# A four-pair opening with two panels side by side in a two-layer hybrid decoder step, on one core

## The chip, the cores and the metric

One core of a Trainium2 chip runs the whole program. The metric is the device time of one execution in microseconds (us); three runs of the kernel before are shown below, and one execution was taken by the profiler.

## What is computed

A decoder trunk of two layers runs one step for 512 prompt tokens and 32 sample tokens (8 sequences of 4). Layer 0 mixes tokens by sliding-window attention with 12 query and 4 key heads, layer 1 by a short gated convolution; in both, 4 further heads attend into 256 memory tokens, and an MLP with a squared ReLU follows. The part that the change touches makes the keys and values of the prompt's memory, for both layers:

```python
def _mem_kv(mem, g, w_kv, k_g):
    n = mem.shape[0]
    kv = _rms_norm(mem, g) @ w_kv
    mk = kv[..., :X_DIM].reshape(n, N_MEM, N_X_HEADS, HEAD_DIM)
    mv = kv[..., X_DIM:].reshape(n, N_MEM, N_X_HEADS, HEAD_DIM)
    return _rms_norm(mk, k_g), mv
```

All inputs are float32 and the products keep nearly that precision: each operand is split into a rounded part (hi) and the rest (lo), and each product is three matmuls (hi·hi, hi·lo, lo·hi).

## The kernel before

Weights stream through a staging buffer `stage` of two places d = 0, 1; a place holds 1,024 KB (8 chunks k of 128 rows by 256 columns). A weight "quad" q is two such loads, so (q, d) names one. ScalarE (ACT) copies a place to `w_hi` (L1389, L1394), VectorE (DVE) subtracts to get `w_lo` (L909 to L912), and the semaphores `w_his[d]` and `w_los[d]` count these. SyncE (SP) issues the next load of a place when `w_los[d]` says that the last one is used up (L449 to L455).

**The opening.** The 256 memory tokens, feature-major in `memx` (8 chunks of 128 by 256), are scaled by the norm's gain and split by `memory_hi` on ACT (L1675) and `memory_lo` on DVE (L1259). Quad 0 holds layer 0's key and value weights, quad 1 those of layer 1. A panel (l, p) of TensorE (PE), in `memory_panel` (L531), is layer l, token half tb = p % 2, and place d = p // 2: p = 0, 1 give keys, p = 2, 3 values. It runs over 8 chunks with three matmuls each, 24 in all, of 256 columns, and adds up in `zps[p % 2][:, 0, 0:256]`, the first of a slot's two banks; so panel p waits (`z_free`) until ACT has taken panel p - 2 out. The norm's factor is left out of the products and multiplied in when a panel is taken: ACT squares the 8 chunks (L1735), DVE adds them in three steps (L1282), PE sums over the partitions in `memory_sums` (L553, called inside panel (0, 0) before its last two chunks), ACT takes the root (L1740), DVE inverts it (L1285), and `take_memory` on ACT (L1687) scales each panel out of its bank.

**The orders written out by hand.** SP issues two loads of memory (512 KB each) and then the two places of quad 0 (L444 to L447). ACT (L1723 to L1766) loads the first part of the constants `con` (44 KB, L1678), converts 8 chunks, copies quad 0's place 0 in two halves, squares 8 chunks, issues the two loads of the tokens `X`, copies place 1, takes the root, and then goes through a loop over (l, p) in which, in this order, each step converts parts of layer 1's memory, brings out finished keys, takes a root of key norms, scales chunks of the tokens (`norm_hi`), takes a panel, copies the next place of weights, and squares tokens. DVE follows with the lo parts in an order of its own (L1268 to L1302). The first engine operation that needs the square root makes ACT load another table of functions. The second part of the constants (443 KB: identity, ones, masks; semaphore `con2`) is issued by ACT after memory's second half has landed (L1728), and PE waits for it before its first panel (L846).

GpSimd (POOL) issues the cached values `vb` when the tokens have landed and the cached keys `kt`, which lie where `memx` lay, after the last use of it (L1886 to L1892). ACT issues the rotary table `cs` in the loop's first step (L1757); POOL needs it for its first rotation (L1893, L1902). SP stores from `vb` (L464, L465) before it goes on with the loads of weights.

After the opening come 12 panels of layer 0's input projection (the first waits for quad 2's `w_los[0]`), attention, the output projection, the MLP, and the same for layer 1.

Of the kernel before, what the change touches and what calls it, by code (L numbers as in the profile page):

```python
# [28 lines left out]
NMEM = 256  # L29
# [37 lines left out]
def build_kernel(nc, xT, memT, wst, cst, rope, swakT, swav, xkT, xv, yT, o_kp, o_vp, o_cp, o_mk, o_mv,  # L67
# [81 lines left out]
    with ExitStack() as ctx:  # L149
# [9 lines left out]
        w_his_half, w_los_half = sem("w_his_half"), sem("w_los_half")  # L159
# [3 lines left out]
        ld = {n: sem("ld_" + n) for n in ("con", "con2", "mem0", "mem1", "x", "x1", "rope", "kt", "vb", "kx0", "kx1", "vx0", "vx1")}  # L163
# [314 lines left out]
        def _(pe):  # L478
# [51 lines left out]

            def memory_panel(l, p):  # L531

                d, tb, slot, q = p // 2, p % 2, p % 2, Q_MEM + l
# [4 lines left out]
                c = l * NMEM + tb * 128  # L538
                for k in range(KC):
                    if (l, p) == (0, 0) and k == KC - 2:  # L540
                        memory_sums()
                    if (l, p) == (0, 0) and k == 0:
                        pe.wait_ge(w_los_half, 1)
                    if (l, p) == (0, 0) and k == KC // 2:
                        pe.wait_ge(w_los[0], 1)
                    if p == 0:
                        pe.wait_ge(m_los[l], k + 1)
                    for i, (w_, r_) in enumerate(((w_hi, 0), (w_hi, 1), (w_lo, 0))):
                        mm = pe.matmul(zps[slot][:, 0, 0:256], act_hl[1][r_][:, k, c:c + 128], w_[:, d, k, :],  # L549
                                       start=(k == 0 and i == 0), stop=(k == KC - 1 and i == 2))  # L550
                mm.then_inc(z_full[slot], 1)

            def memory_sums():  # L553

                pe.wait_ge(m_sum, 3)
# [290 lines left out]
            pe.wait_ge(ld["con2"], 16)  # L846
            for l in range(2):
                for p in range(4):
                    memory_panel(l, p)
# [50 lines left out]
        def _(dve):  # L900
# [1161 lines left out]
```

## Time and profile before

| what | value |
|---|---|
| median of 3 runs | 1170.88 us (1170.84, 1170.88, 1172.97) |
| the profiled execution: its own time | 1172.87 us |
| its span, first to last instruction | 1171.1 us |
| PE busy | 1144.2 us, 98% of the span |
| DVE, ACT, POOL busy | 804.8, 522.4, 132.5 us |
| mean granted TensorE clock | 0.996 |

The profiled execution lies 2.0 us above the median; 1.8 us of it lie outside the span. A difference of 0.2% is 2.3 us.

### The profile page before, as it was taken

The page shows a single profiled execution, that of the slowest core. Times are in us where ns is not written, and L with a number is a line of the kernel's source. Part 1 is how long each engine was busy: PE and PEld are TensorE (multiplying, and loading weights), DVE is VectorE, ACT ScalarE, POOL GpSimd, SP SyncE. Part 2 cuts the span into 40 slices and gives each one's busy share as a digit, 9 for nine tenths or more (in the row PEclk, how much of TensorE's full clock was granted, in tenths as well). Part 3 has the DMA queues.
Part 4 walks back from the last instruction along what each step waited for, and adds up shares of the span by engine and source line. Part 5 has one row for each costly group of instructions (what it writes and reads, how often), then busy time and mean ns, then how long its engine had stood idle before and what let it go on. Part 6 is the DMA issues. An engine that isn't in the chain of part 4 may idle for free.

```text
span 1171.1 us, 22169 instructions
## 1 busy us (share of the span) xinstructions
PE 1144.2 (98%) x8990; PEld 1104.2 (94%) x8990; DVE 804.8 (69%) x1201; ACT 522.4 (45%) x901; POOL 132.5 (11%) x140
## 2 busy tenths in 40 slices
PE   5999899999999999999999999999999999999998
PEld 5899655999999999999999999999999999999998
DVE  6789965798667568558658555589866855856853
ACT  7623767357227326326524222436722722732630
POOL 0038743000000000000141121200000000000000
PEclk9999989999999999999999999999999999999999
DMA  8543150213222312413522322221321332231231
GB/s 333 191 156 118 50 180 1 76 69 114 103 73 102 116 52 91 143 36 108 183 104 73 145 73 73 75 86 59 132 92 66 109 108 72 79 136 39 104 136 48
DMA packets 23146, 120.18 MB, mean 103 GB/s; under 512 B 2708, under 2 KB 6932, under 8 KB 9892
## 3 DMA queue, kind: packets, MB, share of 16 engines
q1 hardware_dynamic: 17892, 100.93, 24.7%
q0 software_dynamic: 1632, 10.54, 2.4%
q10 hardware_dynamic: 3552, 7.74, 1.9%
q8 instruction: 48, 0.79, 0.3%
q14 instruction: 22, 0.18, 0.0%
HBM read 111.29 MB, written 5.69 MB: 100 GB/s over the span
## 4 chain that ended last, share of the span: by engine, by line
PE 88%; DVE 6%; POOL 2%; DMA 2%; ACT 1%; issue 1%; ACTq 1%; DVEq 0%; POOLq 0%
PE zps L498 48%; PE zps L757 25%; PE ops L757 4%; PE zps L745 4%; DVE tmp L974 2%; PE ops L672 1%; PE zps L549 1%; PE tps L642 1%; POOL sm L1874 1%; DVE w_lo L912 1%; DVE sm L1042 1%; DMA tmp<-z 1%; PE zps L596 1%; ACTq L1685 1%; DMA con<-cst 1%
## 5 line engine op out<-in xcount | busy, mean ns | idle before, releaser
L498 PE MATMUL zps<-act_hi,w_hi 128*128 128x272 f32 x1664 | 348.7, 291 | 0.9 <-DVE w_lo L912 0.9
L498 PE MATMUL zps<-act_hi,w_lo 128*128 128x272 f32 x1664 | 344.1, 288 | 0.0
L498 PE MATMUL zps<-act_lo,w_hi 128*128 128x272 f32 x1664 | 343.2, 288 | 0.0
L757 PE MATMUL zps<-xf,wf 128*128 128x272 f32 x2304 | 298.9, 290 | 1.2 <-issue 1.2
L757 PEld LDWEIGHTS zps<-xf,wf 128*128 128x128 f32 x2304 | 294.1, 188 | 1.9 <-issue 1.6
L498 PEld LDWEIGHTS zps<-act_hi,w_hi 128*128 128x128 f32 x1664 | 262.1, 188 | 5.4 <-issue 2.9
L498 PEld LDWEIGHTS zps<-act_lo,w_hi 128*128 128x128 f32 x1664 | 261.5, 189 | 0.0
L498 PEld LDWEIGHTS zps<-act_hi,w_lo 128*128 128x128 f32 x1664 | 260.0, 189 | 0.0
L1387 ACT ACTIVATE w_hi<-w_stage 128x2048 fp32r<-128x2048 f32 (+1 forms) x61 | 114.8, 1883 | 150.8 <-PE zps L498 123.6
L912 DVE TENSOR_TENSOR w_lo<-w_stage,w_hi 128x2048 fp32r<-128x2048 f32 x59 | 137.5, 2331 | 43.2 <-ACT w_hi L1387 43.0
L1387 ACT ACTIVATE wf<-w_sum 128x1024 fp32r<-128x1024 f32 x64 | 67.9, 1061 | 195.2 <-DVE w_sum L930 88.2
L1017 DVE TENSOR_TENSOR tmp<-zps,rstd 128x544 f32<-128x544 f32 x63 | 45.5, 722 | 142.7 <-PE zps L498 116.7
L1874 POOL TENSOR_SCALAR sm<-sm,st 128x256 f32<-128x256 f32 (+2 forms) x55 | 55.0, 1013 | 108.8 <-DVE st L1049 108.7
L1153 DVE TENSOR_TENSOR act_lo<-tmp,act_hi 128x544 fp32r<-128x544 f32 x64 | 46.1, 721 | 20.2 <-ACT act_hi L1387 20.2
L1429 ACT ACTIVATE sm<-sm,st 128x257 f32<-128x257 f32 (+3 forms) x88 | 42.0, 481 | 29.4 <-DVE st L1042 29.4
L1387 ACT ACTIVATE wf<-w_stage 128x1024 fp32r<-128x1024 f32 (+1 forms) x64 | 52.8, 838 | 5.1 <-PE zps L757 5.0
L757 PE MATMUL ops<-xf,wf 128*128 128x272 f32 x384 | 53.7, 289 | 0.0
L757 PEld LDWEIGHTS ops<-xf,wf 128*128 128x128 f32 x384 | 50.4, 188 | 0.0
L943 DVE TENSOR_TENSOR wf<-w_sum,wf 128x1024 fp32r<-128x1024 f32 x32 | 39.2, 1224 | 15.8 <-ACT wf L1387 13.8
L974 DVE RECIPROCAL tmp<-tmp 128x544 f32<-128x544 f32 x12 | 42.6, 3549 | 8.2 <-ACT tmp L1404 8.2
L1247 DVE TENSOR_TENSOR x_res<-tmp,x_res 128x544 f32<-128x544 f32 x63 | 45.7, 726 | 2.2
L1387 ACT ACTIVATE tmp<-zps 128x272 f32<-128x272 f32 x96 | 37.6, 391 | 15.7 <-PE zps L757 14.4
(182 smaller groups left out, 1288.5 us busy)
## 6 DMA issues: line engine op xcount, KB each, us to landing
w_stage<-wst SPq DMA_DIRECT2D x92, 1024.0 KB, 4.9
kx<-xkT POOLq DMA_DIRECT2D x4, 1024.0 KB, 6.4
vx<-xv POOLq DMA_DIRECT2D x4, 1024.0 KB, 6.9
x_res<-xT ACTq DMA_DIRECT2D x2, 1088.0 KB, 7.6
tmp<-z ACTq DMA_DIRECT2D x32, 68.0 KB, 2.1
yT<-x_res ACTq DMA_DIRECT2D x7, 272.0 KB, 2.0
memx<-memT SPq DMA_DIRECT2D x2, 512.0 KB, 4.7
vb<-swav POOLq DMA_DIRECT2D x1, 1024.0 KB, 8.5
```

The costliest lines, as they stand in the source:

```text
L498: mm = pe.matmul(zps[slot][:, h, 0:n], w_[:, d, k, w:w + 128], r_[:, k, c0 + h * n:c0 + (h + 1) * n], start=(j == 0 and i == 0), stop=(j = ...
L745: mm = pe.matmul(zps[slot][:, h, 0:HALF], w_[:, d, k, w:w + 128], r_[:, k, h * HALF:(h + 1) * HALF], start=(k == 0 and i == 0), stop=(k == ...
L757: mm = pe.matmul(bank, wf_hl[pw][:, fw, a, :], x_form(l, px, fx, a)[:, 0, :], start=(begin and a == 0 and j == 0), stop=(a == KC // 2 - 1 ...
L912: dve.tensor_tensor(w_lo[:, d], stage[:, d], w_hi[:, d].bitcast(f32), ALU.subtract).then_inc(w_los[d], 1)
L943: dve.tensor_tensor(w_form(1, W_S3, 2), wsum[:, 2:4], w_form(0, W_S3, 2).bitcast(f32), ALU.subtract).then_inc(w_lo_s34, 1)
L974: link(dve.reciprocal(tmp[:, 3, :], tmp[:, 2, :]))
L1017: dve.tensor_tensor(halves(tmp[:, 0, :]), zp(p % 2), halves(rstd[:, :]), ALU.mult).then_inc(y_mul, 1)
L1153: dve.tensor_tensor(lo[:, m, :], tmp[:, 3 + m % 2, :], hi[:, m, :].bitcast(f32), ALU.subtract).then_inc(u_lo, 1)
L1247: dve.tensor_tensor(X[:, m, :], tmp[:, 0, :], X[:, m, :], ALU.add).then_inc(z_free[p % 2], 1)
L1387: return act.activation(out, in_, ACT.Copy, **kw)
L1429: ins = act.activation(sm[b][:, u, 0:w], sm[b][:, u, 0:w], ACT.Exp, bias=st[:, b, 0, u:u + 1], scale=-1.0, accum_out=st[:, b, 1, u:u + 1])
L1874: ins = pool.tensor_scalar(sm[at][:, u, 0:w], sm[at][:, u, 0:w], st[:, at, 2, u:u + 1], None, ALU.mult)
```

## The change

Memory and quad 0's place 0 come in four pairs of 256 KB transfers (two chunks each), in turn. For each pair ACT converts two chunks of memory, copies two chunks of weights and squares two chunks; DVE follows in step; PE runs the products of both key panels (0, 0) and (0, 1), chunk by chunk, side by side in `first_panels`, and only then the sums. Place 1 of quad 0 is split in two halves, of which DVE makes the first between the first and second of the adds of squares. Panels p = 2, 3 use the slot's second bank, so that no panel of layer 0 waits for a bank, and those of layer 1 wait for the panel two before the one they waited for. PE's wait for `con2` moves behind the first panels. ACT runs one square root on a scrap tile, which POOL has zeroed, before anything has landed. The rotary table is issued in the first step of the input projection, and `vb` behind `kt`.

```diff
@@ SP
-            for i in range(2):
-                sp.dma_start(memx[:, 4 * i:4 * i + 4, :], memT[:, 4 * i:4 * i + 4, :]).then_inc(ld[f"mem{i}"], 16)
-            for d in range(2):
-                sp.dma_start(stage[:, d], wst[d]).then_inc(w_in[d], 16)
+            for i in range(4):
+                c = slice(2 * i, 2 * i + 2)
+                sp.dma_start(memx[:, c, :], memT[:, c, :]).then_inc(ld[f"mem{i}"], 16)
+                sp.dma_start(stage[:, 0, c], wst[0, :, c]).then_inc(ld[f"w{i}"] if i < 3 else w_in[0], 16)
+            sp.dma_start(stage[:, 1], wst[1]).then_inc(w_in[1], 16)
@@ PE
+            def memory_products(l, p, k):
+                d, tb = p // 2, p % 2
+                c = l * NMEM + tb * 128
+                for i, (w_, r_) in enumerate(((w_hi, 0), (w_hi, 1), (w_lo, 0))):
+                    mm = pe.matmul(zps[tb][:, d, 0:256], act_hl[1][r_][:, k, c:c + 128], w_[:, d, k, :],
+                                   start=(k == 0 and i == 0), stop=(k == KC - 1 and i == 2))
+                if k == KC - 1:
+                    mm.then_inc(z_full[tb], 1)
+            def first_panels():
+                for i in range(4):
+                    pe.wait_ge(m_los[0], 2 * i + 2)
+                    if i < 3:
+                        pe.wait_ge(w_los_part, i + 1)
+                    else:
+                        pe.wait_ge(w_los[0], 1)
+                    for p in range(2):
+                        for k in (2 * i, 2 * i + 1):
+                            memory_products(0, p, k)
             def memory_panel(l, p):
-                if p % 2 == 0 and (l, p) != (0, 0):
+                if (l, p) == (0, 2):
+                    pe.wait_ge(w_los_half, 1)
+                elif p % 2 == 0:
                     pe.wait_ge(w_los[d], q + 1)
-                if (l, p) not in ((0, 0), (0, 1)):
-                    pe.wait_ge(z_free[slot], q * 2 + p // 2)
+                if l == 1:
+                    pe.wait_ge(z_free[tb], d + 1)
...
+                    if (l, p) == (0, 2) and k == KC // 2:
+                        pe.wait_ge(w_los[1], 1)
-                    if p == 0:
+                    if (l, p) == (1, 0):
                         pe.wait_ge(m_los[l], k + 1)
+                    memory_products(l, p, k)
             def memory_sums():
+                pe.wait_ge(ld["con2"], 16)
                 pe.wait_ge(m_sum, 3)
...
-            pe.wait_ge(ld["con2"], 16)
+            first_panels()
+            memory_sums()
@@ DVE
-            dve.wait_ge(ld["mem0"], 16)
-            for k in range(KC):
-                memory_lo(0, k)
-            for half, made, done in ((0, w_his_half, w_los_half), (1, w_his[0], w_los[0])):
-                dve.wait_ge(made, 1)
...
+            for i in range(4):
+                c = slice(2 * i, 2 * i + 2)
+                dve.wait_ge(ld[f"mem{i}"], 16)
+                for k in (2 * i, 2 * i + 1):
+                    memory_lo(0, k)
+                if i < 3:
+                    dve.wait_ge(w_his_part, i + 1)
+                else:
+                    dve.wait_ge(w_his[0], 1)
+                dve.tensor_tensor(w_lo[:, 0, c], stage[:, 0, c], w_hi[:, 0, c].bitcast(f32), ALU.subtract).then_inc(
+                    w_los_part if i < 3 else w_los[0], 1)
...
                 dve.tensor_tensor(msq[:, 0:n, :], msq[:, 0:n, :], msq[:, n:2 * n, :], ALU.add).then_inc(m_sum, 1)
-            split_lo(0, 1)
+                if i == 0:
+                    dve.wait_ge(w_his_half, 1)
+                    dve.tensor_tensor(w_lo[:, 1, 0:4], stage[:, 1, 0:4], w_hi[:, 1, 0:4].bitcast(f32), ALU.subtract).then_inc(w_los_half, 1)
+            dve.wait_ge(w_his[1], 1)
+            dve.tensor_tensor(w_lo[:, 1, 4:8], stage[:, 1, 4:8], w_hi[:, 1, 4:8].bitcast(f32), ALU.subtract).then_inc(w_los[1], 1)
...
-            dve.wait_ge(ld["rope"], 16)
@@ ACT
-                copy(key_raw(tb), zps[tb][:, 0, 0:256], scale=mst[:, 2 + tb:3 + tb]).then_inc(z_free[tb], 1)
+                copy(key_raw(tb), zps[tb][:, p // 2, 0:256], scale=mst[:, 2 + tb:3 + tb]).then_inc(z_free[tb], 1)
...
+            act.wait_ge(zeroed, 1)
+            act.activation(tails[:, 0, :], tails[:, 0, :], ACT.Sqrt)
             act.wait_ge(ld["con"], 16)
-            act.wait_ge(ld["mem0"], 16)
...
-            copy(w_hi[:, 0, 0:4], stage[:, 0, 0:4]).then_inc(w_his_half, 1)
-            copy(w_hi[:, 0, 4:8], stage[:, 0, 4:8]).then_inc(w_his[0], 1)
...
+            for i in range(4):
+                c = slice(2 * i, 2 * i + 2)
+                act.wait_ge(ld[f"mem{i}"], 16)
+                for k in (2 * i, 2 * i + 1):
+                    memory_hi(0, k)
+                if i < 3:
+                    act.wait_ge(ld[f"w{i}"], 16)
+                else:
+                    act.wait_ge(w_in[0], 16)
+                copy(w_hi[:, 0, c], stage[:, 0, c]).then_inc(w_his_part if i < 3 else w_his[0], 1)
+                if i == 1:
+                    act.dma_start(con[:, C_IDENT:C_N], cst[:, C_IDENT:C_N]).then_inc(ld["con2"], 16)
+                for k in (2 * i, 2 * i + 1):
+                    act.activation(msq[:, k, :], memx[:, k, :], ACT.Square).then_inc(m_sq, 1)
+                if i > 1:
+                    act.dma_start(X[:, 4 * i - 8:4 * i - 4, :], xT[:, 4 * i - 8:4 * i - 4, :]).then_inc(ld[("x", "x1")[i - 2]], 16)
+            act.wait_ge(w_in[1], 16)
+            copy(w_hi[:, 1, 0:4], stage[:, 1, 0:4]).then_inc(w_his_half, 1)
+            copy(w_hi[:, 1, 4:8], stage[:, 1, 4:8]).then_inc(w_his[1], 1)
             act.wait_ge(ld["con2"], 16)
-            split_hi(0, 1, first=True)
             root(tps[:, :, 0:1], mst[:, 0:2].unsqueeze(2), D, s_full, 1, s_sd, (s_rstd, 1))
...
                 if i == 0:
+                    act.dma_start(cs[:, :, :], rope).then_inc(ld["rope"], 16)
                     root_tokens(2, NT)
@@ POOL
-            pool.wait_ge(ld["x1"], 16)
-            pool.dma_start(vb[:, :, :], swav).then_inc(ld["vb"], 16)
+            pool.memset(tails[:, 0, :], 0.0).then_inc(zeroed, 1)
...
             pool.dma_start(kt[:, :, :, 0:128], swakT).then_inc(ld["kt"], 16)
+            pool.dma_start(vb[:, :, :], swav).then_inc(ld["vb"], 16)
```

## Rows read from the trace of the kernel before

**Rows 1.** Chain of waits, 0 to 115 us: start, length (us), what.
```profile
0.74 4.15 DMA memx<-memT
...
6.53 6.28 DMA con<-cst
...
17.70 9.95 PE zps L549 x78
...
40.17 2.30 DVE w_lo L912
...
42.64 6.24 PE zps L498 x48
...
76.24 1.72 POOL z L1902
```
**Rows 2.** Windows: stretch, its length, busy time of each engine, PEclk, DMA share, GB/s.
```profile
19.07:35.53 16.46, 16.37 (x138) 16.20 (x137) 14.29 (x24) 16.21 (x30) 1.80 (x2) 1.00 0.87 305
...
42.60:125.00 82.40, 82.36 (x623) 80.10 (x624) 71.43 (x57) 30.39 (x43) 41.49 (x26) 1.00 0.42 131
148.00:159.00 11.00, 11.00 (x47) 7.70 (x47) 4.80 (x20) 5.25 (x19) 3.53 (x5) 0.53 0.56 191
```
**Rows 3.** Timeline of ACT, 0 to 20 us: start, length (us), line, operation, count.
```profile
4.96 1.28 ACT L1387 ACT_TABLE_LOAD   x1 [4.96 <-DMA memx<-memT]
...
6.67 2.88 ACT L1387 ACTIVATE act_hi<-memx,con 128x256 fp32r<-128x256 f32 x7
...
10.41 1.04 ACT L1387 ACTIVATE w_hi<-w_stage 128x1024 fp32r<-128x1024 f32 x1
11.36 2.54 ACT L1735 ACTIVATE msq<-memx 128x256 f32<-128x256 f32 x8
13.81 1.90 ACT L1387 ACTIVATE w_hi<-w_stage 128x2048 fp32r<-128x2048 f32 x1
15.73 1.28 ACT L1404 ACT_TABLE_LOAD   x1
17.74 0.26 ACT L1404 ACTIVATE mst<-tps,con 128x2 f32<-128x2 f32 x1 [0.73 <-PE tps L557]
...
19.07 0.47 ACT L1387 ACTIVATE tmp<-zps,mst 128x256 f32<-128x256 f32 x1 [0.28 <-PE zps L549]
```
**Rows 4.** Timeline of DVE, 10 to 17 us.
```profile
10.54 2.36 DVE L1275 TENSOR_TENSOR w_lo<-w_stage,w_hi 128x1024 fp32r<-128x1024 f32 x2 [0.36 <-ACT w_hi L1387]
...
14.00 2.41 DVE L1282 TENSOR_TENSOR msq<-msq 128x1024 f32<-128x1024 f32 x3 [1.02 <-ACT msq L1735]
```
**Rows 5.** DMA issues: count, KB each, median us to landing; then landings of the stage tile.
```profile
con<-cst ACTq DMA_DIRECT2D x1, 44.0 KB, 4.4
yT<-x_res ACTq DMA_DIRECT2D x7, 272.0 KB, 2.0
kt<-swakT POOLq DMA_DIRECT2D x1, 1024.0 KB, 7.0
DMA to landing us min/median/max: 4.9/5.6/10.0
```
**Rows 6.** Timeline of PE, 16 to 39 us.
```profile
16.21 0.41 PE L549 MATMUL zps<-w_hi,act_hi 128*128 128x256 f32 x1
16.43 0.41 PE L549 MATMUL zps<-w_hi,act_lo 128*128 128x256 f32 x1
...
16.86 0.85 PE L557 MATMUL tps<-con,msq 128*128 128x1 f32 x4
...
19.25 0.28 PE L549 MATMUL zps<-w_hi,act_hi 128*128 128x256 f32 x1
19.37 0.28 PE L549 MATMUL zps<-w_hi,act_lo 128*128 128x256 f32 x1
...
38.39 0.38 PE L549 MATMUL zps<-w_hi,act_hi 128*128 128x256 f32 x1 [1.41 <-ACT tmp L1387]
```
**Rows 7.** Timeline of SP, around 58 us.
```profile
58.32 0.61 SPq L465 DMA_DIRECT2D o_vs<-vb  x1
```

More of the change, by code:

```diff
@@ L158, in build_kernel @@
         w_his = [sem(f"w_his{d}") for d in range(2)]
-        w_his_half, w_los_half = sem("w_his_half"), sem("w_los_half")
+        w_his_part, w_los_part, w_his_half, w_los_half = (sem(s) for s in ("w_his_part", "w_los_part", "w_his_half", "w_los_half"))
+        zeroed = sem("zeroed")
         w_los = [sem(f"w_los{d}") for d in range(2)]
@@ L162, in build_kernel @@
         z_free = [sem(f"z_free{s}") for s in range(2)]
-        ld = {n: sem("ld_" + n) for n in ("con", "con2", "mem0", "mem1", "x", "x1", "rope", "kt", "vb", "kx0", "kx1", "vx0", "vx1")}
+        ld = {n: sem("ld_" + n) for n in ("con", "con2", "mem0", "mem1", "mem2", "mem3", "w0", "w1", "w2", "x", "x1", "rope", "kt", "vb", "kx0", "kx1", "vx0", "vx1")}
         m_hi, m_sq, m_los = sem("m_hi"), sem("m_sq"), [sem(f"m_lo{l}") for l in range(2)]
@@ L534, in memory_panel @@
-                if p % 2 == 0 and (l, p) != (0, 0):
+                d, tb, q = p // 2, p % 2, Q_MEM + l
+                if (l, p) == (0, 2):
+                    pe.wait_ge(w_los_half, 1)
+                elif p % 2 == 0:
                     pe.wait_ge(w_los[d], q + 1)
-                if (l, p) not in ((0, 0), (0, 1)):
-                    pe.wait_ge(z_free[slot], q * 2 + p // 2)
-                c = l * NMEM + tb * 128
+                if l == 1:
+                    pe.wait_ge(z_free[tb], d + 1)
@@ L539, in memory_panel @@
                 for k in range(KC):
[L540 to L545, printed above, removed]
-                    if p == 0:
+                    if (l, p) == (0, 2) and k == KC // 2:
+                        pe.wait_ge(w_los[1], 1)
+                    if (l, p) == (1, 0):
@@ L547, in memory_panel @@
                         pe.wait_ge(m_los[l], k + 1)
[L548 to L551, printed above, removed]
+                    memory_products(l, p, k)
             def memory_sums():
+                pe.wait_ge(ld["con2"], 16)
@@ L843, in normed @@
                 return lambda k: (a_los, 4 * n + k + 1)
-            pe.wait_ge(ld["con2"], 16)
+            first_panels()
+            memory_sums()
             for l in range(2):
                 for p in range(4):
-                    memory_panel(l, p)
+                    if (l, p) not in ((0, 0), (0, 1)):
+                        memory_panel(l, p)
                     if p == 3:
@@ L1268, in _ @@
             dve.wait_ge(ld["con"], 16)
-            dve.wait_ge(ld["mem0"], 16)
-            for k in range(KC):
-                memory_lo(0, k)
-            for half, made, done in ((0, w_his_half, w_los_half), (1, w_his[0], w_los[0])):
-                dve.wait_ge(made, 1)
-                c = slice(half * 4, half * 4 + 4)
-                dve.tensor_tensor(w_lo[:, 0, c], stage[:, 0, c], w_hi[:, 0, c].bitcast(f32), ALU.subtract).then_inc(done, 1)
+            for i in range(4):
[9 more added lines that the diff above has]
+                    w_los_part if i < 3 else w_los[0], 1)
             link(dve.tensor_scalar(nsink[:, :], con[:, C_SINK:C_SINK + 16], -1.0, None, ALU.mult))
@@ L1692, in take_memory @@
                 if p >= 2:
-                    copy(memv[:, l, tb, :], zps[tb][:, 0, 0:256], scale=mst[:, 2 + tb:3 + tb]).then_inc(z_free[tb], 1)
+                    copy(memv[:, l, tb, :], zps[tb][:, p // 2, 0:256], scale=mst[:, 2 + tb:3 + tb]).then_inc(z_free[tb], 1)
                     return
@@ L1755, in _ @@
                     norm_hi(0, 4 * l + p, 0)
-                    if (l, p) == (0, 0):
-                        act.dma_start(cs[:, :, :], rope).then_inc(ld["rope"], 16)
                     if (l, p) != (0, 0):
```

12 lines of the change are left out of this document (removed).

## The prediction

> **What bounds the kernel now.** I read the chain of waits first, because it says which work ended last in the opening. It starts with the memory load, goes over the 443 KB of constants that landed at 12.81 us (6.53 + 6.28), and then through 9.95 us of PE's memory panels, a DVE split of weights that ends at 42.47, and PE's first panel of the input projection at 42.64 [rows 1]. The reader is to see two things: PE's first matmul waited for constants that the panels don't use, and the opening ends when DVE has split quad 2's weights, not when PE is done. So I looked next at how busy each engine is between. From 19.07, when ACT takes the first memory panel, to 35.53 ACT works 16.21 of 16.46 us and DVE 14.29 [rows 2]. ACT goes through its list in order there, with 0.25 us of idle time in all; PE's panels are no more than its input. From 42.6 to 125 us PE is busy 82.36 of 82.40 us [rows 2], so whatever the opening gains at 42.64 is kept afterwards.
>
> The question for the change is therefore not when PE starts, but when ACT takes the first panel: at 19.07 before [rows 3]. I call that moment T. From T on, ACT's and DVE's lists are as they were (a DMA issue on ACT's queue aside), and a shift of T shifts the end of the opening by as much.
>
> **The change part by part.** All sums go from the profiled execution (1172.87 us), whose T is 19.07; it stands 2.0 us above the median, 1170.88, and I state the forecast against the median.
>
> *Start, t0.* ACT begins at 4.96 with a table load of 1.28 us and converts its first chunk at 6.26 [rows 3]. The early root loads the table while nothing has landed, and copies and squares ran under that same table later in these rows, so 1.28 us go. What is left is the landing of the first 44 KB of constants (4.4 us after its issue at 0.73, so 5.1) and of the first piece of memory. That piece is halved: 512 KB took 4.15 us [rows 1], and a 272 KB store with rows of 2,176 bytes took 2.0 [rows 5]. So t0 lies between 2.8 (0.74 + 2.0) and 5.15; I take 4.5, nearest the row of the constants, which share the queues with smaller packets now. The Trainium skill, "DMA: Bandwidth & Descriptors", section "Anatomy of one DMA", gives a fixed 2.0 us plus bytes over 436 GB/s, by which 256 KB would land at about 3.35 us, an estimate; the sum below would then be 1169.1, held there by the load of place 1. The trace does not agree: 44 KB took 4.4 us.
>
> *Four pairs on ACT.* Two conversions at 0.41 (2.88 / 7), a copy of 512 columns at 0.53 (half of a step of 0.95 is 0.48, half of a duration of 1.04 is 0.52), two squares at 0.31 (2.45 / 8) [rows 3]: 1.96 us a pair. The last copy of weights starts at t0 + 3 x 1.96 + 0.82 = 11.2 and ends at 11.8; the last square ends at 12.45. DVE's pair is shorter, 2 x 0.41 and half of 1.22 [rows 4], so it follows ACT and is done with place 0 at 12.5.
>
> *First panels on PE.* They start at about t0 + 2.2 = 6.7 instead of 12.85. Matmuls came every 0.22 us early on and every 0.12 us from 19 us [rows 6], which are the two levels of PE's clock, 1.2 and 2.4 GHz. A pair is 12 matmuls, 2.6 us at the low level, 1.4 at the high one. In the rows PE worked 5.7 us before the clock rose; the same here means a rise near 12.4 and the end of both panels by about 15. That is before the sums of squares are ready, so it sets nothing.
>
> *Sums of squares.* DVE's three adds take 2.41 us, and the change puts half a split of place 1 (1.14, the first of two that take 2.36) between the first and second [rows 4]: 12.65 + 2.41 + 1.14 = 16.2. This is later than PE's panels and no earlier than the 16.4 at which the adds ended before (14.00 + 2.41). Here the early start is given back: ACT has copied place 1 by about 14.3 and waits for the root until 16.9, where it had waited only 0.73 us [rows 3].
>
> *Root and first take.* From the sums to the root took 0.88 us from PE's first of the four matmuls, 1.1 with their weight load [rows 6, 3]; at the high clock I take 0.7. Root at 16.9, then 0.16 and two conversions (0.82): T = 17.9. The inversion on DVE, behind the second half of place 1 (16.2 + 1.2), is ready by then.
>
> *Gain:* 19.07 - 17.9 = 1.2 us. **Upper and lower end:** with t0 = 5.15 and the sums at the low clock (0.4 more), T = 18.95, a gain of 0.1. With t0 = 2.8 place 1 takes over: its load landed at 12.1 (issued 2.1, 10.0 to landing [rows 5]) and the same bytes lie ahead of it now; copy 1.04, split 1.14, two adds 1.26, sums 0.7, 0.98 to T and 0.1 of handing over make T = 17.3, a gain of 1.8.
>
> *At nothing:* the second table load (1.28, at 15.73 [rows 3]) vanishes into ACT's wait. The second banks remove PE's wait of 1.41 us at 38.39 [rows 6], but PE then waited again for DVE at 42.64. The rotary table is issued near 47 us and POOL needs it at 76.24 [rows 1]; if that cover were gone, POOL would wait for the transfer. `vb` behind `kt`: both are issued before 42.6, and even at 7.0 us each, one after the other [rows 5], they land by 57, before SP's store from `vb` at 58.32 [rows 7]; SP's weight loads are queued behind that store, so a later `vb` would hold the input projection. The nine issues on SP replace four and run ahead of the data. POOL's zeroing is one small instruction, and only ACT's scrap root waits for it.
>
> **Forecast:** 1170.88 - 1.2 = 1169.7 us.
>
> **Rivals.** *A, PE's lead comes through.* If the 9.95 us of PE on the chain are the bound, what counts is the panels after the sums: PE began panel (0, 2) near 21.7 (27.65 less two panels of 24 matmuls at 0.12) and would begin it at 16.9, 4.8 us sooner: 1166.1. For it speaks the chain, against it ACT's 0.25 us of idle time in 16.46. Chance 0.12.
>
> *B, slower: the small transfers delay place 1.* Its 1,024 KB are issued last on SP's queue, behind eight pieces with rows of 2 KB. Each us of its landing after 12.65 moves T by one. T passes the old 19.07 when it lands after 13.8, and the time passes 0.2% when it lands after 16.2. The slowest row of small packets, `kt` at 1,024 KB in 7.0 us [rows 5], would move the 3,072 KB in 21 us: landing near 22.5, T near 27.8, 1179.6. Against it: 272 KB in 2.0 us with rows as short. Chance 0.07, all of it slower.
>
> *C, PE's clock falls in a new gap.* PE finishes panel (0, 3) near 22.4 and cannot start (1, 0) before DVE has its weights near 26. Before, no such gap was there, and 1.41 us at 38.39 left the spacing as it was [rows 6]; but from 148 to 159 us the granted clock was 0.53 [rows 2], with PE on small attention matmuls. At the low level a panel takes 5.2 instead of 2.9 us; the four panels have 15.3 us and need 12.2 at the high level, so some 6 us of low clock are hidden, and a stretch of 10.5 us, as in that row, costs 2.1: 1171.8. The Trainium skill, "TensorE: Matmul & The Clock Gate", section "What's actually happening", says that the default state is throttled and that activity releases it, which speaks against a change that only runs PE ahead of its feeders; the fall at 148 us agrees with it. Chance 0.09, nearly all of it no change.
>
> **How the numbers follow.** The main case has 0.72: gains from 0.1 to 1.8, so 1169.1 to 1170.8 against the median. The runs before scatter by 2.1 us (1170.84 to 1172.97); I estimate that the low-clock stretch at 148 us, which need not be there in each run, is a part of that, so the range goes up to 1172.6. Down it goes to 1168.2, since gains may add that I have not seen; A and B lie outside it. A measurement tells 0.2%, 2.3 us, from no change. Faster than that: A, and 0.07 of the main case with its ends in the right direction, 0.19. Slower: B and a small part of C, 0.09. Within it: 0.72.
>
> **What would show it right or wrong.** Right: PE's first matmul near 6.7, the adds ending near 16.2, ACT idle for over 2 us ahead of the root, the first take near 17.9, the first panel of the input projection near 41.4, PE idle before panel (1, 0). Wrong: a first projection panel before 40 us (A), place 1's copy on ACT after 12.7 (B), matmuls every 0.22 us between 26 and 41 (C), or the same 41.4 with the gain lost after it, which would say that the stages behind are tied to a transfer or to the clock.

## The result, and the profile after

The changed kernel is slower: 1173.68 us median of 12 runs (1170.62 to 1177.97) beside 1170.89 of the kernel before, ratio 1.0025 with a 95% interval of 1.0014 to 1.0036. In a later set of runs it took 1174.33 us beside 1170.97, ratio 1.0015 (0.9998 to 1.0032). I had forecast 1169.7 and within 0.2%. The profiled execution of the changed kernel took 1171.89 us with a span of 1170.1, which is less than the 1172.87 of the profiled execution before; why a slower kernel can show a shorter profile is part of the reading.

I read the chain of waits first, as before; its columns are start, length in us, and what. Of the changed kernel:

```profile
4.50 9.82 DMA w_stage<-wst
...
43.05 7.78 PE zps L500 x48
...
130.79 0.66 PE ops L594 x4
...
199.02 48.32 PE zps L500 x384
```

And two later pieces of the same chain of the kernel before, which answer to the last two:

```profile
128.92 0.66 PE ops L575 x4
...
200.30 48.32 PE zps L498 x384
```

The chain of before began with memory, constants and PE's panels [rows 1]. After, it begins with one transfer: place 1 of the staged weights, issued at 4.50 and landed at 14.32. The first panel of the input projection starts at 43.05 where it had started at 42.64, and takes 7.78 us where it had taken 6.24 [rows 1]: what follows it starts 0.41 + 1.54 = 1.95 us later. At the four transposes ahead of the attention the delay is still 1.87 us (130.79 against 128.92). Then it turns over: at the long projection block the changed kernel is 1.28 us ahead. The granted clock says why. These windows of the changed kernel have the columns of [rows 2]:

```profile
43.05:46.60 3.55, 3.55 (x17) 3.55 (x18) 2.99 (x7) 1.47 (x4) 0.00 (x0) 0.54 0.69 226
46.60:50.83 4.23, 4.23 (x35) 4.23 (x35) 3.08 (x3) 2.53 (x4) 0.00 (x0) 0.98 0.51 196
50.83:125.00 74.17, 74.17 (x560) 71.91 (x559) 63.40 (x43) 24.52 (x28) 39.99 (x25) 1.00 0.42 131
...
126.00:166.00 40.00, 36.60 (x283) 22.59 (x281) 31.82 (x118) 30.21 (x112) 24.73 (x47) 0.96 0.34 110
```

The first projection panel ran at 0.54 until 46.6, that is at the low level of 1.2 GHz, and PE was then saturated up to 125, so the loss stayed. Over the attention of the first layer, 126 to 166 us, the clock was 0.96; the same window of the kernel before:

```profile
126.00:166.00 40.00, 36.55 (x258) 22.36 (x258) 29.21 (x114) 28.18 (x103) 22.88 (x42) 0.87 0.33 110
```

The profiled execution of before happened to hold a low stretch [rows 2] that the one of after has in smaller part, and 3.15 us were won there (1.87 + 1.28). I take that for scatter between executions and no part of the change: the runs of the kernel before differ among themselves by as much (below), and in the means of the runs the changed kernel is behind and not ahead. So the loss that the trace shows is what stands at 51 us: 1.95 us, beside 2.9 and 2.2 us between the means of the two sets of runs (1173.88 against 1170.97, and 1173.92 against 1171.73; each difference has a standard error of 0.6 to 0.7 us).

Now the opening. SP's issue of place 1 and ACT in the changed kernel, to be read beside [rows 3] (start, length, line, operation, what ended the idle time before it):

```profile
4.50 0.58 SPq L449 DMA_DIRECT2D w_stage<-wst  x1
```

```profile
4.55 0.91 ACT L1415 ACTIVATE act_hi<-memx,con 128x256 fp32r<-128x256 f32 x2 [1.87 <-DMA con<-cst]
...
14.34 2.00 ACT L1415 ACTIVATE w_hi<-w_stage 128x1024 fp32r<-128x1024 f32 x2 [1.53 <-DMA w_stage<-wst]
...
18.54 0.26 ACT L1432 ACTIVATE mst<-tps,con 128x2 f32<-128x2 f32 x1 [2.20 <-PE tps L576]
18.70 0.90 ACT L1415 ACTIVATE act_hi<-memx,con 128x256 fp32r<-128x256 f32 x2
19.50 0.46 ACT L1415 ACTIVATE tmp<-zps,mst 128x256 f32<-128x256 f32 x1
```

DVE, beside [rows 4]:

```profile
13.04 1.23 DVE L1307 TENSOR_TENSOR msq<-msq 128x1024 f32<-128x1024 f32 x1
15.43 1.23 DVE L1310 TENSOR_TENSOR w_lo<-w_stage,w_hi 128x1024 fp32r<-128x1024 f32 x1 [1.17 <-ACT w_hi L1415]
16.57 1.14 DVE L1307 TENSOR_TENSOR msq<-msq 128x512 f32<-128x512 f32 x2
17.64 1.22 DVE L1312 TENSOR_TENSOR w_lo<-w_stage,w_hi 128x1024 fp32r<-128x1024 f32 x1
```

PE, beside [rows 6]:

```profile
6.85 0.55 PE L538 MATMUL zps<-w_hi,act_hi 128*128 128x256 f32 x1 [6.85 <-DVE w_lo L1299]
...
17.86 0.58 PE L576 MATMUL tps<-con,msq 128*128 128x1 f32 x4 [2.52 <-DVE msq L1307]
...
27.72 0.39 PE L538 MATMUL zps<-w_hi,act_hi 128*128 128x256 f32 x1 [1.73 <-DVE w_lo L933]
...
39.45 0.38 PE L586 MATMUL ops<-con,tmp 128*128 128x128 f32 x2
43.05 0.55 PE L500 MATMUL zps<-act_hi,w_hi 128*128 128x272 f32 x2 [3.22 <-DVE w_lo L933]
```

The first steps came as forecast: ACT starts at 4.55, PE's first matmul is at 6.85. Then DVE does one add, stands idle for 1.17 us because place 1 is late, splits half of it, and only then goes on with the two adds on which the root waits. The first take is at 19.50, 0.43 us later than before [rows 3]. PE, freed by the second banks, is done at 39.8, stands idle for 3.22 us where it had stood idle for 0.9, and its clock falls as it comes out of the gap.

The clock of the changed kernel falls once more, earlier: PE stands idle for 2.52 us ahead of the sums, and soon after it runs panel (0, 2) at the low level.

```profile
19.40:22.80 3.40, 3.40 (x18) 3.40 (x18) 2.44 (x6) 3.37 (x9) 0.00 (x0) 0.50 0.99 381
```

This stretch costs no time, because the take of that panel on ACT comes later anyway, but with the stretch at 43 us it takes 0.003 off the mean clock of the execution. None of the changed kernel's 24 runs shows more than 0.996, so its mean clocks are not to be set beside those of the kernel before.

### The profile page after: what moved, and what is told of

It reads as the page before. It is cut to its first block, busy times and chain, and to the rows that moved or that the text cites. A ratio compares the mean times of both kernels' runs of the same rounds, so it can differ in the third digit from the quotient of the medians.

```text
span 1170.1 us, 22186 instructions
## 1 busy us (share of the span) xinstructions
PE 1144.2 (98%) x8990; PEld 1104.6 (94%) x8990; DVE 805.2 (69%) x1204; ACT 521.4 (45%) x904; POOL 132.6 (11%) x141
## 4 chain that ended last, share of the span: by engine, by line
PE 87%; DVE 6%; ACT 2%; POOL 2%; DMA 2%; issue 1%; ACTq 1%; SPq 0%; DVEq 0%; POOLq 0%
PE zps L500 48%; PE zps L776 25%; PE ops L776 4%; PE zps L764 4%; DVE tmp L995 2%; PE ops L691 1%; PE tps L661 1%; POOL sm L1907 1%; DVE w_lo L933 1%; DMA w_stage<-wst 1%; DVE sm L1063 1%; DMA tmp<-z 1%; PE zps L615 1%; ACT w_hi L1415 1%; ACTq L1713 1%
## 5 line engine op out<-in xcount | busy, mean ns | idle before, releaser
L1415 ACT ACTIVATE w_hi<-w_stage 128x2048 fp32r<-128x2048 f32 (+2 forms) x64 | 115.3, 1804 | 152.5 <-PE zps L500 123.6
L964 DVE TENSOR_TENSOR wf<-w_sum,wf 128x1024 fp32r<-128x1024 f32 x32 | 39.2, 1225 | 16.2 <-ACT wf L1415 14.2
```

Of the source, the lines that this page charges most:

```text
L964: dve.tensor_tensor(w_form(1, W_S3, 2), wsum[:, 2:4], w_form(0, W_S3, 2).bitcast(f32), ALU.subtract).then_inc(w_lo_s34, 1)
L1415: return act.activation(out, in_, ACT.Copy, **kw)
```

## The experiments

A first panel of the projection at the high clock takes 6.24 to 6.26 us in every profile here, so "panel start + length" against the 48.88 us of before (42.64 + 6.24) tells what the opening is worth; the time of a run holds much more scatter. The mean clock of an execution tells how much: of the kernel before, 35 runs on one chip, those at 0.999 took 1169.0 to 1170.1 us, those at 0.996 1171.2 to 1172.8, four at 0.991 1176.9 to 1177.0. Twelve runs of one kernel have a standard deviation near 2 us, their mean one of about 0.6. I therefore put the opening of each profile beside the means. The kernel before on the chips of these runs has means of 1171.83, 1171.81 and 1171.73.

| kernel | first take | panel start + length | opening against before | mean of 12 against before |
|---|---|---|---|---|
| changed kernel, first and again | 19.50, 19.54 | 43.05 + 7.78, 43.08 + 7.78 | +1.95, +1.98 | +2.91, +2.20 |
| adds first | 17.81 | 41.36 + 7.78 | +0.26 | +1.02 |
| first banks alone, and again | 18.64, 19.47 | 42.20 + 6.26, 43.01 + 6.26 | -0.42, +0.39 | +2.48, +1.19 |
| before with second banks | 18.89 | 42.45 + 8.75 | +2.32 | +0.86 |
| gap filled | 19.39 | 42.93 + 6.24 | +0.29 | +1.31 |
| adds first, first banks, and again | 18.27, 17.74 | 42.34 + 6.26, 41.81 + 6.26 | -0.28, -0.81 | +0.44, -0.21 |
| adds first, gap filled | 18.10 | 42.17 + 6.26 | -0.45 | +0.98 |
| before with the moves alone | 19.17 | 43.15 + 6.24 | +0.51 | -0.40 |
| X later (one run) | 21.08 | 45.24 + 7.80 | +4.16 | |
| pieces of 512 KB (one run) | 18.91 | 42.45 + 9.01 | +2.58 | |

**The order on DVE (e1).** The half split of place 1 goes behind the three adds.

```
                 dve.tensor_tensor(msq[:, 0:n, :], ...).then_inc(m_sum, 1)
-                if i == 0:
-                    dve.wait_ge(w_his_half, 1)
-                    dve.tensor_tensor(w_lo[:, 1, 0:4], ...).then_inc(w_los_half, 1)
+            dve.wait_ge(w_his_half, 1)
+            dve.tensor_tensor(w_lo[:, 1, 0:4], ...).then_inc(w_los_half, 1)
```

> The changed kernel with the first half of place 1's split on DVE moved behind the three adds of squares. In the changed kernel ACT's first take of a panel is at 19.50 us, because the adds wait 1.17 us for place 1's copy and run 1.14 us behind its split. Theory L (the late take: what moves ACT's first take moves the whole opening): the adds end near 15.4, the first take comes near 18.0, the first projection panel near 41.5 instead of 43.05, and the time falls by 1.5 us against the changed kernel, to 1172.2. Theory C (the clock: PE runs out of work 3.2 us before the first projection panel and starts it at 1.2 GHz) expects the same gain of 1.5 but the panel still at 7.8 us, since PE's gap is as long. If the stages behind the take were not tied to it, the first projection panel stays at 43.

Measured: 1172.84 us median, ratio 1.0006 (0.9988 to 1.0024). ACT:

```profile
13.85 2.01 ACT L1414 ACTIVATE w_hi<-w_stage 128x1024 fp32r<-128x1024 f32 x2 [1.12 <-DMA w_stage<-wst]
16.19 0.26 ACT L1431 ACTIVATE mst<-tps,con 128x2 f32<-128x2 f32 x1 [0.34 <-PE tps L576]
16.35 0.90 ACT L1414 ACTIVATE act_hi<-memx,con 128x256 fp32r<-128x256 f32 x2
17.81 0.47 ACT L1414 ACTIVATE tmp<-zps,mst 128x256 f32<-128x256 f32 x1 [0.56 <-DVE mst L1313]
```

The idle time ahead of the root shrinks from 2.20 to 0.34 us, the first take comes 1.69 us earlier and so does the first projection panel (41.36 against 43.05). The chain from the take to that panel is rigid, 23.55 us here as in the changed kernel and 23.57 before. Not all of the 1.69 us is the order on DVE: place 1 was 0.49 us earlier in this run (13.85 against 14.34). With the order of the changed kernel the take lay 5.15 to 5.16 us behind the start of place 1's copy in six profiles, whose copies start between 13.48 and 14.75 (changed kernel and its repeat, e2, g2, e4, q2; 5.57 in q3 and q4); here it lies 3.96 us behind, and 3.62 in f3, f4 and g3. So T goes with place 1, and the order on DVE, with place 1 late, cost 1.2 to 1.5 us of it. PE's gap shrinks as well, and the panel still takes 7.78 us:

```profile
41.36 0.49 PE L500 MATMUL zps<-act_hi,w_hi 128*128 128x272 f32 x2 [1.85 <-DVE w_lo L933]
```

Its first matmuls still ran at the high level, and the clock fell within it:

```profile
42.80:46.20 3.40, 3.40 (x17) 3.40 (x16) 3.15 (x7) 2.75 (x5) 0.00 (x0) 0.50 0.93 345
```

A gap of 1.85 us could be followed by the low clock, then, as one of 1.73 before panel (1, 0) in the changed kernel was not; idle time alone does not decide it.

**The second banks (e2, e3) and the gap (e4).** e2 is the changed kernel with the first bank of each slot alone and the waits of before; e3 is the kernel before with nothing but the second banks; e4 is the changed kernel with 24 matmuls of no use in the gap.

```
# e2, on the changed kernel (e3 is the reverse, on the kernel before)
-                if l == 1:
-                    pe.wait_ge(z_free[tb], d + 1)
+                pe.wait_ge(z_free[tb], q * 2 + d)
...
-                    mm = pe.matmul(zps[tb][:, d, 0:256], act_hl[1][r_]...
+                    mm = pe.matmul(zps[tb][:, 0, 0:256], act_hl[1][r_]...
# e4, ahead of the first projection panel
+            pe.wait_ge(s_sd, 1)
+            for j in range(24):
+                pe.matmul(tps[:, 0, 0:256], act_hl[1][0][:, j % KC, 0:128], act_hl[1][0][:, j % KC, 0:256], start=True, stop=True)
```

> The changed kernel with the first bank of each slot alone and the old waits for it. Theory C: panel (1, 3) waits again for ACT's take, ends near 42, PE's gap before the first projection panel shrinks from 3.2 to about 1 us, the panel takes 6.2 instead of 7.8 us, and the time falls by 1.6 to 2.4 us against the changed kernel, to between 1171.3 and 1172.1; the first projection panel still starts near 43.0. Theory L alone: the first take is still at 19.5, so nothing changes, 1173.7.

> The kernel before with the second bank for panels 2 and 3, and nothing else of the change. Theory C: PE ends panel (1, 3) near 39.5 instead of 41.3, waits about 3 us for quad 2's weights, and the first projection panel takes up to 7.8 instead of 6.2 us: slower than before by up to 1.6 us, 1172.4. Theory L alone: the first take stays at 19.07, the first projection panel at 42.64, and the time stays at 1170.9.

> The changed kernel with 24 matmuls of no use (128x256, into a bank that is free then) between PE's last memory panel and the first projection panel, 2.9 us at 2.4 GHz, so that PE's gap before it is nearly full. Theory C: the first projection panel still starts near 43.05 but takes 6.2 instead of 7.8 us, and the time falls by 1.6 to 2.4 us, to between 1171.3 and 1172.1. Theory L alone: no change, 1173.7; if the matmuls run over, up to 0.5 us more.

Measured: 1173.69 us (ratio 1.0021, 1.0005 to 1.0037), 1171.96 (1.0001, 0.9982 to 1.0020) and 1173.05 (1.0011, 0.9994 to 1.0029). PE of e2, of e3 and of e4 at the first projection panel:

```profile
42.20 0.49 PE L500 MATMUL zps<-act_hi,w_hi 128*128 128x272 f32 x2 [0.91 <-DVE w_lo L932]
42.53 0.41 PE L500 MATMUL zps<-act_lo,w_hi 128*128 128x272 f32 x2
```

```profile
42.45 0.79 PE L498 MATMUL zps<-act_hi,w_hi 128*128 128x272 f32 x2 [3.22 <-DVE w_lo L912]
43.04 0.66 PE L498 MATMUL zps<-act_lo,w_hi 128*128 128x272 f32 x2
```

```profile
39.49 3.09 PE L878 MATMUL tps<-act_hi 128*128 128x256 f32 x24
42.93 0.49 PE L500 MATMUL zps<-act_hi,w_hi 128*128 128x272 f32 x2 [0.36 <-DVE w_lo L936]
43.26 0.41 PE L500 MATMUL zps<-act_lo,w_hi 128*128 128x272 f32 x2
```

With the first banks alone PE's gap is 0.91 us as before, and two matmuls take 0.41 us. With the second banks on the old kernel, without anything else of the change, the gap is 3.22 and two matmuls take 0.66; with the gap filled it is 0.36 and they take 0.41. In e3 the clock fell while PE still stood idle, and stayed low for longer:

```profile
41.20:48.00 6.80, 5.55 (x24) 5.58 (x25) 5.52 (x10) 5.04 (x9) 0.00 (x0) 0.50 0.46 158
```

So the second banks make the gap, the fall comes with it, and the price in these profiles is 1.5 us (7.78 against 6.24) to 2.5 (8.75). The Trainium skill, "TensorE: Matmul & The Clock Gate", section "What's actually happening", says that the clock is throttled by default and that activity releases it; the trace agrees, with 0.54 behind 3.22 us of idle time and 1.00 behind 0.36.

As times these three were misses. By its opening e2 is 0.4 us ahead of the kernel before; its mean lay 2.5 us behind. Its attention, in the window that had 0.87 before:

```profile
126.00:166.00 40.00, 36.60 (x233) 20.89 (x231) 27.68 (x105) 27.07 (x99) 19.35 (x38) 0.74 0.25 84
```

It caught far more of the low clock there than the others. And e3, whose profile lost 2.3 us in the opening, had runs at 1169.3 and 1169.7 with a mean clock of 0.999, as low as nearly any of the kernel before. A stretch of 6.8 us at half the clock takes 0.003 off that mean by itself, so the fall in that gap does not come in every execution.

**A quiet base that was none (q1 to q4).** To take the scatter out I put matmuls of no use into the attention of the first layer, in four kernels alike, so that the clock should hold there.

```
+            def keep_busy(out):
+                pe.matmul(out, ones, con[:, C_IDENT:C_IDENT + 256], start=True, stop=True)
```

> The kernel before with one matmul of no use ahead of each pair of transposes of layer 0's attention and three ahead of each of the two products of the sample heads, to keep PE's clock up there: runs of the kernel before scatter from 1169.0 to 1177.0 us with their mean granted clock (0.999 to 0.991), and the profile shows the low stretches in the attention. If that scatter is the attention's clock, the mean clock is 0.999 in nearly all runs and the times lie within about 1 us of each other, near 1169.3 plus what the added matmuls cost (up to 5 us where PE is the bound there). If it is not, the scatter stays. This kernel is the base for the next three.

> The changed kernel with the same added matmuls. Theory C (clock in PE's gap before the first projection panel, on top of a first take 0.4 us late): 1.9 us above the steady kernel before, with a first projection panel of 7.8 us where the clock fell, and two groups of runs if it does not fall in each. Theory L (late take alone): 0.4 us above it. Theory A (the shift by 0.4 to 2 us changes the attention's clock and nothing else): no difference between the steady kernels.

> The changed kernel with the first banks and the old waits alone, and the added matmuls. Theory C: no gap, a first projection panel of 6.2 us, so within 0.5 us of the steady kernel before and 1.5 us below the steady changed kernel. Theory L: as the steady changed kernel, 0.4 us above the steady kernel before. If instead it is above the steady changed kernel, the second banks gain something that the profiles so far do not show.

> The changed kernel with PE's gap filled by 24 matmuls of no use, and the added matmuls. Theory C: 1.5 us below the steady changed kernel, 0.4 us above the steady kernel before. Theory L: as the steady changed kernel.

Medians: 1184.97, 1185.73, 1183.83 and 1188.33 us of 4 or 5 runs each. The added matmuls cost about 14 us on the kernel before, and profiles of q1, q2 and q4 still hold 6.8 us and more at the low clock in the attention, so as a base this failed and the times decide nothing. The first projection panels repeat the reading above: 6.26 us in the one built on before, 7.77 in the one built on the changed kernel, 6.26 with first banks alone, 6.24 with the gap filled.

**Why place 1 is late (f1, f2).** Two suspects: the activations X, issued at 9.5 and 10.9 us instead of after the squares, and the small packets. f1 moves X's issues behind the landing of place 1; f2 puts the eight small transfers together to four of 512 KB in the same order (the waits for them on ACT and DVE, not shown, follow suit). Both were profiled in one run each.

```
# f1
-                if i > 1:
-                    act.dma_start(X[:, 4 * i - 8:4 * i - 4, :], ...)
             act.wait_ge(w_in[1], 16)
+            for i in range(2):
+                act.dma_start(X[:, 4 * i:4 * i + 4, :], ...)
# f2
-            for i in range(4):
-                c = slice(2 * i, 2 * i + 2)
+            for i in range(2):
+                c = slice(4 * i, 4 * i + 4)
                 sp.dma_start(memx[:, c, :], memT[:, c, :])...
                 sp.dma_start(stage[:, 0, c], wst[0, :, c])...
```

> The changed kernel with its two issues of the activations (X) moved from 9.5 and 10.9 us to behind the landing of place 1, so that nothing but the constants' second part shares the queues with place 1. Theory X (the activations take the queues from place 1): place 1's copy on ACT starts at 12.0 to 12.8 instead of 14.34, and the first take comes about 1.7 us earlier, near 17.8, unless the later X becomes the wait in front of it. Theory P (the pairs in small packets are slow from the beginning, 2551 KB moved by 10 us against 2985 KB before): place 1's copy still starts after 13.5. Either way PE's gap before the first projection panel stays over 2 us and that panel takes 7.8 us.

> The changed kernel with the eight transfers of the opening's pairs put together to four of 512 KB with rows of 4 KB, in the same order; place 1 and X stay as they are. Theory P (small packets): place 1's copy on ACT starts at 12.2 to 13.0 instead of 14.34, though the first conversion comes later than 4.55, and the first take lies near 18. Theory X: place 1's copy still starts after 13.8 and the take near 19.3. PE's gap before the first projection panel and its 7.8 us stay under both.

The chain of waits of f1 has the transfer of place 1, and ACT its copy:

```profile
4.50 10.30 DMA w_stage<-wst
```

```profile
15.68 2.00 ACT L1415 ACTIVATE w_hi<-w_stage 128x1024 fp32r<-128x1024 f32 x2 [2.34 <-DMA w_stage<-wst]
```

The same copy in f2:

```profile
13.39 1.99 ACT L1415 ACTIVATE w_hi<-w_stage 128x1024 fp32r<-128x1024 f32 x2
```

Without X on the queues place 1 is no earlier: it landed at 14.80 against 14.32, and its copy started later still because my edit put X's two issues in front of it. With pieces of 512 KB, issued at 2.85, it landed 10.1 us later, at 12.95, before ACT asked for it at 13.39; the copy lies between the two bounds that I had written down. The throughput of the DMA queues, every 0.3 us from 3 to 15, shows where the time goes; the kernel before, the changed kernel, f2:

```profile
GB/s 277 374 324 345 421 440 396 382 382 341 437 382 355 437 437 437 437 437 437 410 437 382 437 375 454 405 420 445 428 478 395 464 406 406 464 464 435 406 406 435
```

```profile
GB/s 159 165 384 358 382 396 382 410 376 348 239 102 164 205 321 321 382 410 458 437 478 430 457 418 385 391 500 384 396 435 423 407 487 406 445 418 418 464 464 435
```

```profile
GB/s 224 339 313 294 379 414 437 396 382 410 369 328 273 300 273 341 423 437 382 437 451 437 437 426 419 430 380 412 484 453 418 368 442 406 464 435 464 464 435 435
```

All three mostly move some 350 to 480 GB/s once they run. The changed kernel starts at 160 and has a hole from 6.0 to 7.2 us, down to 102; f2's hole reaches 273, and before has none. So X is not the cause, and the cut into small pieces is the likely one; it rests on one profile of f2 (12.95) against landings from 13.5 to 14.8 with the small pairs, and on the throughput. Which side of the cut delays place 1 stays open. The rows are shorter, and place 1 is issued later, at 4.50 instead of 2.1, because nine issues of 0.4 to 0.6 us stand on SP's queue instead of four; f2 changed both. Against the late issue as the whole cause speaks that the last of the nine was out at 5.1 (4.50 + 0.58), before the hole opens; why it opens just there I can show and not explain. f2 did not gain by its earlier place 1 all the same: its first conversion is at 5.33, its adds start at 13.7, its take is at 18.91, and its first projection panel took 9.01 us where I had written 7.8. In f1 PE's gap was 1.82 us, where I had written over 2, and the panel took 7.80.

**Both losses taken out (f3, f4, and f3 again as g3).** f3 is e1 with e2, f4 is e1 with e4.

> The changed kernel with both of its losses taken out: the half split of place 1 behind the three adds, and the first banks alone. By my theory the first take lies at 17.2 to 17.9, the first projection panel starts at 40.8 to 41.4 and takes 6.25 us; that is 1.2 to 1.8 us before the kernel before and 3.2 to 3.8 before the changed one, at an equal clock in the attention: 1169 to 1170 us for the median, ratio 0.9985 to 0.999. If instead the opening does not reach the end, the time stays at 1171 to 1173 with the panel at 41.

> The changed kernel with the half split of place 1 behind the three adds, both banks kept, and 24 matmuls of no use in PE's gap before the first projection panel. By my theory the same as with the first banks alone: take at 17.8, first projection panel at 41.4 and 6.25 us long, 1169 to 1170 us for the median, ratio 0.9985 to 0.999. If the second banks cost by something else than the clock in that gap, this kernel stays 1 us or more behind the one with the first banks alone.

> The changed kernel with the half split behind the adds and first banks alone, a second time: mean 1171.5 to 1172.7 by scatter and opening, no more than 1 us from the first-banks-alone kernel beside it.

Measured: 1172.07 us (ratio 1.0002, 0.9989 to 1.0015), 1172.07 (1.0012, 0.9999 to 1.0025), and again 1171.05 (1.0002, 0.9985 to 1.0019). These are as fast as the kernel before and not faster; my 1169 to 1170 was a miss. The panel lengths are 6.26, but the openings win only 0.3 to 0.8 us, and ACT of g3 shows why:

```profile
14.12 2.00 ACT L1413 ACTIVATE w_hi<-w_stage 128x1024 fp32r<-128x1024 f32 x2 [1.52 <-DMA w_stage<-wst]
...
17.74 0.47 ACT L1413 ACTIVATE tmp<-zps,mst 128x256 f32<-128x256 f32 x1 [0.62 <-DVE mst L1312]
...
22.18 1.91 ACT L1413 ACTIVATE w_hi<-w_stage 128x2048 fp32r<-128x2048 f32 x1 [0.40 <-DMA w_stage<-wst]
```

Now the next place of weights lands at 22.2 and ACT waits for it: with T near 17.8 the stream of weights is the bound, and 0.4 of the gain is given back to it. Nor can T fall much further there, since the take waits for DVE's reciprocal behind all of DVE's adds and splits.

**The moved fetches (g1), and the repeats (g2, g4).** g1 is the kernel before with the rotary table (its lines are not shown) and `vb` issued late, and nothing else; g2 is e2 again, g4 the changed kernel again.

```
-            pool.wait_ge(ld["x1"], 16)
-            pool.dma_start(vb[:, :, :], swav).then_inc(ld["vb"], 16)
...
             pool.dma_start(kt[:, :, :, 0:128], swakT).then_inc(ld["kt"], 16)
+            pool.dma_start(vb[:, :, :], swav).then_inc(ld["vb"], 16)
```

> The kernel before with the moved fetches alone: the rotary table issued at the first projection panel, vb behind kt. My theory: nothing hangs on them, the first projection panel starts at 42.3 to 43.0 and takes 6.25 us, and the time is that of the kernel before within 0.7 us, ratio 0.9994 to 1.0006. The rival, that the later fetches cost in the projection stage: 1 us or more above, with VectorE's, ScalarE's and TensorE's rows shifted against the kernel before somewhere between 45 and 130 us.

> The changed kernel with the first banks alone, a second time. If only scatter lay between its time (mean 1174.3) and its opening (panel at 42.2, 6.26 us long, 0.4 us before the kernel before), its mean is now 1171 to 1173; if the pairs and side-by-side panels cost after the opening, it is again above 1173.5.

> The changed kernel itself, beside these: first projection panel at 42.7 to 43.5 and 7.8 us long, 1.5 to 2.5 us above the kernel before in the mean, and about 2 us above the kernel with first banks alone.

Measured: 1171.18 us (ratio 0.9994, 0.9981 to 1.0007), 1172.56 (1.0013, 0.9999 to 1.0028) and 1174.33. The moves cost nothing that can be measured in the time; in g1's profile the first projection panel starts at 43.15, a little behind the 42.3 to 43.0 that I had written. The changed kernel repeats itself to 0.04 us in its take and its mean. The kernel with the first banks alone came down by 1.4 us in the mean, from 1174.31 to 1172.92: most of its miss was scatter, and it is now 1.0 us below the changed kernel beside it, where I expected 2, and 1.4 above g3, where I expected no more than 1.

What stays open: in the table the variants of the changed kernel lie 0.6 to 1.4 us (e2 the first time 2.9) above what their opening says, the two variants of the old kernel 0.9 to 1.5 below. Of the former, 0.3 us is a loss near 840 us that every one of their profiles has and the old kernel's have not (told of at the end). For the rest, clocks and collisions scatter by more than that, so I leave it unsettled whether a further small cost after the opening remains.

## Why the prediction was wrong

**Two steps failed, one of 1.6 us and one of 1.5: the bound on place 1, and the second banks, booked at nothing.** First place 1. I took its landing as 12.1, as before, because "the same bytes lie ahead of it now". They did, but they moved more slowly, and the nine issues on SP, booked as running "ahead of the data", put its own issue from 2.1 to 4.50: it landed at 14.3, and between 13.5 and 14.8 us in the other kernels with the small pairs. With that one value my own working holds: the text gave T one us later for each us of landing after 12.65, so 17.9 + (14.3 - 12.65) = 19.55; measured 19.50. Had I asked what halves and quarters of transfers had cost anywhere, the only rows were 44 KB in 4.4 us and 272 KB in 2.0 [rows 5]; I set the second against rival B, though it was a single store and no row of eight pieces in turn.

**Rival B was the mechanism of this first step**, at 0.07 much too low a chance for its mechanism; the size that the chance stood for, a landing after 16.2, did not come. It moved T past the old value, 0.43 us, as "after 13.8" had said, and this alone would not have been measured.

**Rival C was right in kind and wrong in place.** I looked for the clock's fall in the gap before panel (1, 0), where it is hidden: there the gap was 1.73 us in the changed kernel and the clock stayed at 1.00 behind it. The hidden fall of the changed kernel came at 19.4 instead, after PE's wait for the sums; in e1 it came before panel (1, 0), at the place I had named, and was hidden as well. Of the second banks I wrote that they remove a wait of 1.41 us at 38.39 and that PE then waits for DVE, and booked this at nothing. The wait did go, PE did wait for DVE, and the two idle times (1.41 and 0.91 us) gave way to one of 3.22 us, behind which the first panel of a saturated stage ran at the low clock. The term booked at 0 was 1.54. This gap did no harm by its idle time, only by the clock behind it, and it stood just ahead of 82 us in which PE is the bound [rows 2]. The prediction also lets the row at 148 us agree with the rule that activity releases the clock; that row has PE busy for 11.00 of 11.00 us by the profile, with 47 matmuls, at 0.53, so it does not show the rule by itself.

**What held, and what did not.** t0: 4.5, measured 4.55. The formula set beside it, from the Trainium skill, "DMA: Bandwidth & Descriptors", section "Anatomy of one DMA", stands there for transfers that GpSimd issues, and these are issued by SP and ACT; no term of the sum hung on it. PE's first matmul: 6.7, measured 6.85. The end of the adds: 16.2, measured 17.64, late with place 1. Sums to root: 0.7, measured 0.90. Root to take: 0.98, measured 0.96. T as the thing that counts for the panel's start: a shift of 1.69 in T shifted it by 1.69 (e1). The moves at nothing: g1. Rival A did not come: ACT stayed the bound. The gain of 1.2 that I forecast was there to be had in part: with the adds first and the first banks the take is at 17.74, but the next weights then hold ACT.

**The sum with both terms:** +0.43 for T (+0.41 at the panel) and +1.54 for its length, 1.95 us or 0.17%; the means of two sets of runs say 2.9 and 2.2.

## What to carry to other kernels

A transfer that was cut small to let the first consumer start sooner was paid for here by the last piece in the queue, 2.2 us later: look for who waits for that one, and put work that does not need it ahead of the wait in the engine's list. When a wait is removed from an engine that will wait anyway, add up its idle time ahead of the next stage that it bounds: PE's gaps of 1.41 and 0.91 us cost nothing here, those of 1.85 and 3.22 us ahead of the saturated stage cost 1.5 us and more. Where runs scatter by more than the change is worth, compare a point inside the trace (here the start and length of one panel), not the end times, and only then ask the means.

## What the runs showed that was not expected

VectorE and GpSimd collide where the kernel has them both work on the rotary embedding, and which of them starts first decides who pays. DVE and then POOL around the last block ahead of the attention, first in the changed kernel:

```profile
122.15 0.79 DVE L997 SCALAR_TENSOR_TENSOR z<-z,con,tmp 128x544 f32<-128x544 f32 x1
...
122.57 1.59 POOL L1935 TENSOR_TENSOR z<-z,cs 128x544 f32<-128x544 f32 x1
```

and in e4:

```profile
121.05 1.83 DVE L1000 SCALAR_TENSOR_TENSOR z<-z,con,tmp 128x544 f32<-128x544 f32 x1
...
120.94 1.36 POOL L1938 TENSOR_TENSOR z<-z,cs 128x544 f32<-128x544 f32 x1
122.26 1.84 POOL L1939 TENSOR_TENSOR tmp<-tmp,cs 128x544 f32<-128x544 f32 x1
```

Where DVE starts first it takes 0.79 us and POOL's next instruction 1.59; where POOL starts 0.11 us ahead, DVE takes 1.83. What follows on DVE came 1.04 us later in e4, counted from the start of that instruction. The Trainium skill, "SBUF — State Buffer", section "Who interferes with whom", says that a DVE instruction with two inputs in SBUF contends with a GpSimd instruction that reads it, and that issue order decides who blocks; the rows agree. The ten instructions of this form up to 135 us sum to 9.2 to 11.7 us in the profiles taken, so by my estimate this alone can move an execution by some 2 us.

In every profile of the changed kernel and of its variants from e1 to g4, and in neither e3 nor g1, another 0.3 us is lost between 755 and 848 us, far from the change (in f3 near 840 us, where PE pauses and waits for nothing that the profile shows); its cause was not tried.
